# Key and value projections of a two-layer decode step: three one-pass products in place of one fp32 product

## The chip, the cores and the metric

The kernel runs on one core of one Trainium2 chip, as one program. The metric is the device time of one execution in microseconds (us). The engines are TensorE (PE in the profile, its weight loads PEld), VectorE (DVE), ScalarE (ACT), GpSimd (POOL) and SyncE (SP, which here only issues DMAs).

## What is computed

One inference step of a decoder with two layers: a convolution layer, then an attention layer with three branches (compressed, selected, window). There are 512 prompt tokens and 64 sample tokens (8 sequences of 8), so 576 rows of width 1024. Between the layers one key/value set is projected, and that is what the change touches:

```python
def kv_rows(x, g_kv, w_kv):
    h = rms_norm(x, g_kv)
    kv = (h @ w_kv).reshape(x.shape[0], x.shape[1], N_BRANCH, 2, KV_HEADS, HEAD_DIM)
    return kv[:, :, 0], kv[:, :, 1], kv[:, :, 2]
```

`w_kv` is 1024 x 1536: three branches, each 256 columns of keys and 256 of values. The rows of branch 0 are then compressed (windows of 32 tokens through a small network), the keys of branches 1 and 2 are transposed for the scores, all rows are outputs too.

## The kernel before

The program is written by hand, one stream of instructions per engine; the engines wait for each other on counting semaphores, and each executes strictly in its written order. The stages on TensorE are: input projections of the convolution layer (lines 1779 to 1799), statistics and the compression of the past (1801 to 1835), the output projection `row_product` (1871 to 1885), the key/value stage (1888 to 1940), compression of the new rows and first tiles of the query/gate projection (1942 to 1976), the attention loop (2059 to 2070) and the end (2073 to 2171).

**Two kinds of matrix product.** Operands typed fp32 go through `product` (line 1679); an fp32 matmul appears in the trace as two records. The large projections of both layers are done in another way: each operand is split into a high part (an ACT copy into a tile typed fp32r) and a low part (whole minus high, on DVE or POOL, in place), and three fp32r matmuls are added: high x high, high x low, low x high (`split_rows`, lines 1693 to 1701). An fp32r matmul appears as one record.

**The key/value stage.** `w_kv` comes in six chunks of 256 columns (1 MB each): chunk c belongs to branch c // 2, keys where c is even, values where odd. There are five row groups t: four of 128 prompt tokens, and t = 4 with the 64 sample tokens. Job n (loop of line 1899) is one chunk and one row group: 8 fp32 matmuls with 128 stationary token columns of `hT` and 256 moving columns of the chunk, into a half bank of PSUM. In branch 0 the tokens are taken with a step of two. The two t = 4 jobs of a branch are done together (line 1922). The order is by branch, then chunk, then row group; ten jobs per branch, thirty in all. ACT copies each result out of PSUM (line 978), starts the output DMAs after each branch (989 to 997), and at n = 10 copies `u_hi`. PE may run six jobs ahead of these copies.

**The transposes.** `kt_transposes(br)` turns the keys of a branch (two 128x128 transposes per row group, into banks 6 and 7 in turn); branch 1 comes behind job 23, branch 2 behind the last job. Then come 16 transposes of the compressed branch's rows (`ctp_tr`, line 1936), which DVE copies into `ctP` (line 1410), and then `compress_p(0, 1)`, which waits for `ctp_ready` 4 and `kv_ready` 30.

**What comes before.** For each t, `row_product(t)` (four chunks of 8 fp32 matmuls) is followed by a chain over ACT and DVE: squares, root, scale, residual, squares, root, `xn_b` (lines 911 to 937 and 1340 to 1377). PE turns `xn_b` of row group t-1 behind the product of t (`turn_b`), and DVE makes `hT` and `uT` from it (line 1365).

**Loads.** SP issues the weight chunks in one fixed order (line 525 on) and waits before each until its place is free. Chunks 0 and 1 of `w_kv` lie in places 4 and 5 of a ring of six; chunks 2 to 5 take places that hold the output projection's weights, so SP waits for `o_mm` 5, the end of `row_product(4)`. The first query/gate tiles take the places of `w_kv` chunks in turn.

Of the kernel before, what the change touches and what calls it, by code (L numbers as in the profile page):

```python
# [27 lines left out]
P = 128  # L28
# [39 lines left out]
def build(nc, I, O):  # L68
    ctx = ExitStack()
    with ctx:  # L70
# [66 lines left out]
        hT = at(R_H, KD, NT)  # L137
# [18 lines left out]
        scaled_b = at(R_F + 4096, D)  # L156
# [9 lines left out]
        ctP = at(R_G, 2, 8, KV, 32)  # L166
# [14 lines left out]
        wgate_hi = over("wgate_hi", R_Z + 3200, KD, 48)  # L181

        k_stage = at(R_Z, 2, TT, CH)
# [102 lines left out]

        def rows_slot(n):
# [45 lines left out]
        def kv_at(c, t):  # L333


            return 10 * (c // 2) + (4 * (c % 2) + t if t < 4 else 8 + c % 2)
# [43 lines left out]
        for n in range(6):  # L380
            last_use[C_KV + n] = ("kv_mm", kv_at(n, 4) + 1)
# [12 lines left out]
        kv_jobs = {kv_at(c, t): (c, t) for c in range(6) for t in range(TT)}  # L394
# [16 lines left out]
        def chunk_sb(c):  # L411
            return ring[:, place[c][0] // (2 * D)]
# [18 lines left out]
        def rows(t):  # L431
            return P if t < 4 else NS

# [54 lines left out]
        def _(sp):  # L488
# [96 lines left out]
            def new_v_rows(n):  # L585
                b, br = n // 2, n % 2
                sp.dma_start(vnew[:, n % 6], v_sb[NS + DS * b:NS + DS * b + DS, br, 4, :]).then_inc(slot_in[n % 6], 16)
# [38 lines left out]
        def _(pool):  # L626
# [64 lines left out]
            for kind in range(2):  # L691
                for b in range(DB):
                    pool.dma_start(O["win_sample"][b, PAST:KS, kind].rearrange("t k d -> t (k d)"),
                                   (v_sb if kind else k_stage)[kind * NS + DS * b:kind * NS + DS * b + DS, 1, 4]).then_inc(S["late"], 16)
# [44 lines left out]
        def _(act):  # L739
# [170 lines left out]

            for t in range(TT):
# [30 lines left out]
            def split_hi(j):  # L942

                if j == 1:
                    act.wait_ge(S["wg_in"], 16)
                    act.wait_ge(S["o_mm"], TT)
                    copy(wgate_hi, wgate).then_inc(S["hi_ready"], 1)
                    return
                i = j - (j > 1)
                act.wait_ge(slot_in[i % TRING], arrived[C_Q + i])  # L950
                if i >= HRING:
                    act.wait_ge(S["tile_mm"], tile_done(i - HRING))
                copy(tile_hi[:, i % HRING], tile_w[:, i % TRING]).then_inc(S["hi_ready"], 1)

            for n in range(30):
                br, (c, t) = n // 10, kv_jobs[n]
                kind = c % 2
                if n == 10:
# [8 lines left out]
                p0 = kind * NS if t == 4 else 0  # L967
                here = slice(p0, p0 + rows(t))
                act.wait_ge(S["kv_mm"], n + 1)
                src = pb(kv_bank(n), CH)[here]  # L970
                if br == 0 and t < 4:
                    dst = cmp_rows[:, t // 2, kind, :, HD * (t % 2):HD * (t % 2) + HD]
                    src = src.rearrange("p (k d) -> p k d", d=HD)
                elif br == 0:
                    dst = cmp_rows_s[here, kind * CH:(kind + 1) * CH]
                else:
                    dst = (v_sb if kind else k_stage)[here, br - 1, t]
                copy(dst, src).then_inc(S["kv_ready"], 1)
                if n % 10 < 9:
                    continue  # L980

                act.wait_ge(S["kv_ready"], n + 1)
                for kind in range(2):
                    here = slice(kind * NS, kind * NS + NS)
# [11 lines left out]
                    if br == 1:  # L996
                        act.dma_start(O["slc_sample"][:, :, kind].rearrange("b t k d -> (b t) (k d)"), R[here, 0, 4]).then_inc(S["kv_out"], 16)
            split_hi(2)
# [201 lines left out]
        def _(dve):  # L1200
# [138 lines left out]

            for t in range(TT + 1):  # L1340
# [15 lines left out]
                if t:  # L1356
# [7 lines left out]
                    for q, T in enumerate((hT, uT)):  # L1364
                        V.tensor_tensor(out=T[:, :, k * P:k * P + rk], in0=pb(4 + 2 * (k % 2), KD, P)[:, :, 0:rk],
                                        in1=gain(4 + q, rk), op=ALU.mult).then_inc(S["hu_ready"], 1)
                if t < TT:
# [8 lines left out]
                    if t == 1:  # L1376
                        sample_scale()

            def split_lo(j):

                dve.wait_ge(S["hi_ready"], C_OA + j + 1)
# [4 lines left out]
                V.tensor_tensor(out=tile_lo[:, j % TRING], in0=tile_w[:, j % TRING], in1=tile_hi[:, j % HRING],  # L1386
# [7 lines left out]

            for n in range(2 * TT):
                if n == TT:
                    split_lo(0)
                    split_lo(1)
# [7 lines left out]
            dve.wait_ge(S["cs_mm"], 6)  # L1406
            for n in range(4):
                c, gi = n // 2, n % 2
                dve.wait_ge(S["ctp_tr"], n + 1)
                V.tensor_copy(ctP[:, c, :, :, 16 * gi:16 * gi + 16].rearrange("p j k c -> p k c j"),  # L1410
                              pb(6 + n % 2, KV, 16, 8)).then_inc(S["ctp_ready"], 1)
# [262 lines left out]
        def _(pe):  # L1674
# [34 lines left out]
            def tile_product(b0, j):  # L1709
                i = j - (j > 1)  # L1710
                pe.wait_ge(S["lo_ready"], j + 2)
                return split_product(b0, tile_hi[:, i % HRING], tile_lo[:, i % TRING])
# [175 lines left out]
            def kt_transposes(br):  # L1888
                for t in range(TT):
                    n = TT * br + t  # L1890
                    r = rows(t)
                    pe.wait_ge(S["kv_ready"], kv_at(2 * br + 2, t) + 1)
                    if n >= 2:
                        pe.wait_ge(S["kt_ready"], n - 1)
                    for p in range(2):
# [3 lines left out]
            for n in range(30):  # L1899
                c, t = kv_jobs[n]  # L1900
                await_chunk(C_KV + c)
# [10 lines left out]
                if t < 4:  # L1912
                    if c < 2:
                        lhs = hT[:, :, (t // 2) * 256 + t % 2:(t // 2) * 256 + 256:2]
                    else:
                        lhs = hT[:, :, t * P:(t + 1) * P]
                    product(pb(kv_bank(n), CH), ((lhs[:, k], chunk_sb(C_KV + c)[:, k]) for k in range(KD))).then_inc(S["kv_mm"], 1)
                elif c % 2:

                    for k in range(KD):  # L1920
                        for kind in range(2):
                            ins = pe.matmul(pb(kv_bank(n - 1 + kind), CH, p0=kind * NS, p1=kind * NS + NS), hT[:, k, SEQ:NT],
                                            chunk_sb(C_KV + c - 1 + kind)[:, k], start=(k == 0), stop=(k == KD - 1))
                            if k == KD - 1:
                                ins.then_inc(S["kv_mm"], 1)
                if n == 23:
                    kt_transposes(0)
            kt_transposes(1)
            for n in range(4):
                c, gi = n // 2, n % 2  # L1930
                if n >= 2:
                    pe.wait_ge(S["ctp_ready"], n - 1)
                else:
                    pe.wait_ge(S["kt_ready"], 2 * TT)
                for kv in range(KV):
                    ins = pe.transpose(pb(6 + n % 2, KV, P)[:, kv], cmp_rows[:, gi, c, kv], ident)
                ins.then_inc(S["ctp_tr"], 1)

            pe.wait_ge(S["kv_ready"], 30)
# [10 lines left out]
            compress_p(0, 1)  # L1950
            pe.wait_ge(S["hidp_ready"], 2)
# [9 lines left out]
            pe.wait_ge(S["lo_ready"], 3)  # L1961
# [16 lines left out]
            def tile_part(part):  # L1978
# [4 lines left out]
                for k in ks:  # L1983
                    if k == 0:
                        if (i, hf) in bank_clear:
                            pe.wait_ge(S[bank_clear[i, hf][0]], bank_clear[i, hf][1])
                        pe.wait_ge(S["lo_ready"], i + 3)
                    w_hi, w_lo = tile_hi[:, i % HRING, k], tile_lo[:, i % TRING, k]
# [214 lines left out]
```

## Time and profile before

| | us |
|---|---|
| three runs | 987.19, 990.16, 990.83 (median 990.16) |
| the profiled execution's own time | 992.36 |
| its span in the trace | 990.5 |
| PE / DVE / ACT / POOL busy | 923.6 / 511.0 / 424.1 / 302.2 |
| mean granted TensorE clock | 0.986 of full speed |

The profile shows one execution; the trace gives each instruction's start and duration in us from the start of the span. A chain view follows the work that ended last back to what released it; along it, a stretch of matmuls is shown with the time by which they advance. The record of a single matmul is longer than the distance between two, since they are pipelined; the distance is what counts.

### The profile page before, as it was taken

To read this page: it belongs to the slowest core of one execution; us is meant where nothing else is said; L and a number is where in the kernel's file an instruction comes from. 1 tells how busy PE (TensorE), PEld (TensorE's weight loads), DVE (VectorE), ACT (ScalarE), POOL (GpSimd) and SP (SyncE) were. 2 spreads that over 40 slices of the span, in tenths; PEclk is the share of its full clock that TensorE was granted. 3 is DMA by queue.
4 is the path that set the end of the run, shared out by engine and by line. 5 is a ranking of instruction groups with operands and counts; after the bars stand their busy time and mean duration, and the time that the engine had idled before them with its cause. 6 is when DMAs were issued, how large, how long until landed. Compare 5 with 4: busy or idle time off the path is not lost.

```text
span 990.5 us, 16977 instructions
## 1 busy us (share of the span) xinstructions
PE 923.6 (93%) x6398; PEld 788.4 (80%) x6398; DVE 511.0 (52%) x1162; ACT 424.1 (43%) x884; POOL 302.2 (31%) x311
## 2 busy tenths in 40 slices
PE   2799999998999999998989999999999999799996
PEld 2699999944379878876988988989898989686663
DVE  2477999965842450212224545554555545635553
ACT  4456676623412321211334555554554645523411
POOL 0269888771460000003002333233232323400000
PEclk9999999999999999999989999999999999999997
DMA  8345442157336142234532232222232100922521
GB/s 213 85 111 164 117 113 76 49 173 260 143 103 227 43 147 64 48 96 108 133 87 43 65 65 66 43 65 46 62 87 44 44 1 15 269 93 89 170 76 32
DMA packets 156071, 97.44 MB, mean 98 GB/s; under 512 B 97156, under 2 KB 144932, under 8 KB 155911
## 3 DMA queue, kind: packets, MB, share of 16 engines
q1 hardware_dynamic: 141134, 77.07, 29.2%
q0 software_dynamic: 4896, 10.32, 3.0%
q10 hardware_dynamic: 9961, 8.97, 2.7%
q8 instruction: 52, 0.85, 0.4%
q14 instruction: 28, 0.23, 0.1%
HBM read 87.48 MB, written 18.85 MB: 107 GB/s over the span
## 4 chain that ended last, share of the span: by engine, by line
PE 83%; DVE 4%; ACT 4%; SPq 4%; DMA 3%; issue 2%; ACTq 0%; POOL 0%; DVEq 0%
PE psum L1679 17%; PE psum L1989 7%; PE psum L1698 6%; PE psum L1699 6%; PE psum L1700 6%; PE psum L1990 6%; PE psum L1991 6%; PE psum L2084 5%; PE psum L2054 4%; PE psum L2019 3%; PE psum L2037 3%; PE psum L1771 3%; ACT arena L1124 2%; SPq L531 2%; DMA arena<-in_cmp_w 2%
## 5 line engine op out<-in xcount | busy, mean ns | idle before, releaser
L1679 PE MATMUL psum<-arena 128*128 128x256 f32 (+2 forms) x832 | 168.9, 364 | 1.2 <-issue 1.2
L1679 PEld LDWEIGHTS psum<-arena 128*128 128x128 f32 (+1 forms) x832 | 144.8, 187 | 22.6 <-issue 2.3
L741 ACT ACTIVATE arena<-psum 128x512 f32<-128x512 f32 (+9 forms) x214 | 83.6, 434 | 167.5 <-PE psum L1679 59.1
L1989 PE MATMUL psum<-u_hi,tile_hi 128*128 128x288 f32 x464 | 146.5, 316 | 8.6 <-ACT arena L741 8.4
L720 POOL TENSOR_SCALAR arena<-arena,kept 128x512 f32<-128x512 f32 (+3 forms) x128 | 83.6, 668 | 181.7 <-DVE kept L1545 181.7
L1990 PE MATMUL psum<-u_lo,tile_hi 128*128 128x288 f32 x464 | 137.9, 297 | 0.0
L1991 PE MATMUL psum<-u_hi,tile_lo 128*128 128x288 f32 x464 | 137.0, 295 | 0.0
L1273 DVE SCALAR_TENSOR_TENSOR psum<-arena,psum 128x512 f32<-128x512 f32 x168 | 127.0, 756 | 6.0
L1698 PE MATMUL psum<-h_hi,tile_hi 128*128 128x288 f32 x384 | 115.0, 299 | 4.1 <-DVE tile_lo L1245 4.1
L1699 PE MATMUL psum<-h_lo,tile_hi 128*128 128x288 f32 x384 | 114.5, 298 | 0.0
L1700 PE MATMUL psum<-h_hi,tile_lo 128*128 128x288 f32 x384 | 114.1, 297 | 0.0
L1989 PEld LDWEIGHTS psum<-u_hi,tile_hi 128*128 128x128 f32 x464 | 87.7, 189 | 19.8 <-ACT arena L741 11.4
L1476 DVE COPY arena<-psum 128x512 f32<-128x512 f32 (+3 forms) x72 | 37.0, 514 | 103.1 <-PE psum L2037 100.3
L1124 ACT ACTIVATE arena<-arena,kept 128x512 f32<-128x512 f32 (+3 forms) x128 | 70.4, 551 | 44.5 <-DVE kept L1511 44.5
L1990 PEld LDWEIGHTS psum<-u_lo,tile_hi 128*128 128x128 f32 x464 | 87.9, 189 | 1.7 <-issue 1.7
L1991 PEld LDWEIGHTS psum<-u_hi,tile_lo 128*128 128x128 f32 x464 | 87.6, 189 | 0.0
L1698 PEld LDWEIGHTS psum<-h_hi,tile_hi 128*128 128x128 f32 x384 | 73.2, 191 | 4.2 <-issue 4.2
L1699 PEld LDWEIGHTS psum<-h_lo,tile_hi 128*128 128x128 f32 x384 | 73.5, 191 | 0.0
L1700 PEld LDWEIGHTS psum<-h_hi,tile_lo 128*128 128x128 f32 x384 | 73.4, 191 | 0.0
L644 POOL TENSOR_TENSOR tile_lo<-tile_whole,tile_hi 128x1024 fp32r<-128x1024 f32 x23 | 56.4, 2450 | 29.4 <-ACT tile_hi L741 29.3
L741 ACT ACTIVATE tile_hi<-tile_whole 128x1024 fp32r<-128x1024 f32 x56 | 59.1, 1056 | 6.5 <-PE psum L1700 5.5
L2084 PE MATMUL psum<-arena 128*128 128x256 f32 x256 | 60.2, 386 | 1.3 <-POOL arena L727 1.3
(271 smaller groups left out, 1565.2 us busy)
## 6 DMA issues: line engine op xcount, KB each, us to landing
tile_whole<-in_b_w_in SPq DMA_DIRECT2D x64, 256.0 KB
tile_whole<-in_a_w_in SPq DMA_DIRECT2D x24, 512.0 KB
arena<-in_cmp_w SPq DMA_DIRECT2D x3, 2048.0 KB, 10.1
arena<-in_w_kv SPq DMA_DIRECT2D x6, 1024.0 KB, 12.1
bias_copies<-bias_line POOLq DMA_DIRECT2D x4, 1280.0 KB, 25.2
arena<-in_x_prompt SPq DMA_DIRECT2D x8, 512.0 KB, 10.5
arena<-in_a_w_out SPq DMA_DIRECT2D x4, 1024.0 KB, 16.7
arena<-bias_copies SPq DMA_DIRECT2D x16, 256.0 KB, 3.6
```

The source lines that it names most:

```text
L720: pool.tensor_scalar(L, L, rden[:, stat(n) + k:stat(n) + k + 1], gR[:, i, h:h + 1], ALU.mult, ALU.mult).then_inc(S["pn_ready"], 1)
L741: return nc.scalar.activation(out, in_, ACT.Copy, scale=scale)
L1124: nc.scalar.activation(L, L, ACT.Exp, scale=-1.0, bias=mn[:, k:k + 1], accum_out=den[:, k:k + 1]).then_inc(S["exp_done"], 1)
L1273: V.scalar_tensor_tensor(out=acc_p, in0=glu_p[:, m, w:w + SEQ], scalar=tap, in1=acc_p, op0=ALU.mult, op1=ALU.add).then_inc(S["conv_step"], 1)
L1679: ins = pe.matmul(out, l, r, start=(k == 0), stop=(k == len(pairs) - 1))
L1698: pe.matmul(out, w_hi[:, k], h, start=(k == 0), stop=False)
L1699: pe.matmul(out, w_hi[:, k], l, start=False, stop=False)
L1700: ins = pe.matmul(out, w_lo[:, k], h, start=False, stop=(k == KD - 1))
L1989: pe.matmul(pb(7, HT), w_hi, u_hi[:, k, here], start=(k == 0), stop=False)
L1990: pe.matmul(pb(7, HT), w_hi, u_lo[:, k, here], start=False, stop=False)
L1991: ins = pe.matmul(pb(7, HT), w_lo, u_hi[:, k, here], start=False, stop=(k == KD - 1))
L2084: ins = pe.matmul(pb(4 + 2 * (t % 2), 4, CH)[:, c], yT[:, k, t * P:(t + 1) * P], chunk_sb(C_OB + c)[:, k], start=(k == 0), stop=(k == KD - 1))
```

## The change

- **Products.** A job is now a whole branch (keys and values, 512 moving columns, one full bank) and one row group: 15 jobs, n = 5 x branch + t. Each has for each of the 8 slices of the contraction three fp32r matmuls. The sample rows are no longer done in pairs; keys and values both lie in partitions 0 to 63.
- **Splits.** `hT` becomes `kvh_whole`; ACT makes `kvh_hi`, DVE `kvh_lo`, one row group at a time, inside the loop over the output projection's row groups. Each chunk of `w_kv` (128 x 2048 words) is split the same way: chunks 0 and 1 in iterations t = 2 and 3 of that loop, 2 and 3 at n = 1 and 2 of ACT's copy loop, 4 and 5 at n = 6 and 7.
- **Places.** The high parts lie where `x_sb` was (branch 1), and at the end of R_F and start of R_G (branches 0 and 2). `ctP`, `scaled_b`, `k_stage`, `wgate_hi` and the slots of `tile_hi` move; chunks 2 to 5 now lie in places 0 to 3 in order.
- **Order.** The 16 transposes of compressed rows go behind jobs 5 and 6, the key transposes two groups each behind jobs 11 to 14, the last two behind `compress_p(0, 1)`. ACT's copies `u_hi` move behind ten of the fifteen jobs, DVE's tile splits ahead of the key copies. `compress_p(0, 1)` waits for `kv_ready` 24 and `ctp_ready` 4.

```diff
@@ places
-                i = (4, 5, 3, 0, 1, 2)[c - C_KV] if C_KV <= c < C_Q else c % RING if c < C_KV else c - C_OB
+                i = (4, 5, 0, 1, 2, 3)[c - C_KV] if C_KV <= c < C_Q else c % RING if c < C_KV else c - C_OB
@@ ScalarE
+            def kv_rows_hi(t):
+                act.wait_ge(S["hu_ready"], 2 * (t + 1))
+                act.wait_ge(S["o_mm"], t + 1)
+                here = slice(t * P, t * P + rows(t))
+                copy(kvh_hi[:, :, here], kvh_whole[:, :, here]).then_inc(S["hh_ready"], 1)
+
+            def kv_weight_hi(c):
+                act.wait_ge(place[C_KV + c][2], arrived[C_KV + c])
+                if c >= 4:
+                    act.wait_ge(S["kv_mm"], 5)
+                copy(kvw_hi(c // 2)[:, c % 2], kvw_whole[:, (4, 5, 0, 1, 2, 3)[c]]).then_inc(S["hi_ready"], 1)
...
+                if t >= 2:
+                    kv_rows_hi(t - 2)
+                if t in (2, 3):
+                    kv_weight_hi(t - 2)
+            kv_rows_hi(TT - 2)
+            kv_rows_hi(TT - 1)
...
+            for n in range(3 * TT):
+                br, t = n // TT, n % TT
+                if n == 1:
                     act.wait_ge(S["x1_out"], 16 * TT)
                     act.wait_ge(S["xn_b_ready"], TT)
-                    act.wait_ge(S["hu_ready"], 2 * TT)
+                if n in (1, 2):
+                    kv_weight_hi(n + 1)
+                if n in (6, 7):
+                    kv_weight_hi(n - 2)
+                if n == 2 * TT:
+                    act.wait_ge(S["kv_mm"], 2 * TT)
                     for m in range(KD):
                         copy(u_hi[:, m], uT[:, m]).then_inc(S["uh_ready"], 1)
-                if n == 24:
+                if n == 12:
                     split_hi(0)
                     split_hi(1)
...
@@ VectorE
+                    if t >= 2:
+                        kv_rows_lo(t - 2)
+                    if t in (2, 3):
+                        kv_weight_lo(t - 2)
+                    if t == TT - 1:
+                        kv_rows_lo(TT - 2)
+            kv_rows_lo(TT - 1)
+            for c in range(2, 4):
+                kv_weight_lo(c)
+            for n in range(4):
+                c, gi = n // 2, n % 2
+                dve.wait_ge(S["ctp_tr"], n + 1)
+                V.tensor_copy(ctP[:, c, :, :, 16 * gi:16 * gi + 16].rearrange("p j k c -> p k c j"),
+                              pb(6 + n % 2, KV, 16, 8)).then_inc(S["ctp_ready"], 1)
+            for c in range(4, 6):
+                kv_weight_lo(c)
...
@@ TensorE
+            def three(out, w, x, first, last):
+                pe.matmul(out, w[0], x[0], start=first, stop=False)
+                pe.matmul(out, w[0], x[1], start=False, stop=False)
+                return pe.matmul(out, w[1], x[0], start=False, stop=last)
+
+            for n in range(3 * TT):
+                br, t = n // TT, n % TT
+                pe.wait_ge(S["lo_ready"], 1 + 2 * br + 2)
                 if n == 2:
                     turn_b(TT - 1)
                 if n < 2:
-                    pe.wait_ge(S["hu_ready"], 2 * (n + 1))
                     pe.wait_ge(S["o_scaled"], 4)
                 elif n < 6:
-                    pe.wait_ge(S["hu_ready"], 2 * TT if n >= 4 else 2 * (n + 1))
                     pe.wait_ge(S["o_scaled"], TT)
+                    pe.wait_ge(S["hu_ready"], 2 * TT if n >= 4 else 8)
                 else:
-                    pe.wait_ge(S["kv_ready"], n - 5)
...
+                    pe.wait_ge(S["kv_ready"], 2 * (n - 5))
+                if n < 5:
+                    pe.wait_ge(S["hl_ready"], TT + (2, 2, 4, 4, 5)[n])
+                r = rows(t)
+                tokens = slice((t // 2) * 256 + t % 2, (t // 2) * 256 + 256, 2) if br == 0 and t < 4 else slice(t * P, t * P + r)
+                for k in range(KD):
+                    ins = three(pb(kv_bank(n), 2, CH)[0:r], [h[:, k, tokens] for h in (kvh_hi, kvh_lo)],
+                                [w[:, :, k] for w in (kvw_hi(br), kvw_lo(br))], k == 0, k == KD - 1)
+                ins.then_inc(S["kv_mm"], 1)
+                if n in (5, 6):
+                    ctp_transposes(range(2 * n - 10, 2 * n - 8))
+                if n >= 11:
+                    kt_transposes(range(2 * n - 22, 2 * n - 20))
+            pe.wait_ge(S["kv_ready"], 24)
             pe.wait_ge(S["ctp_ready"], 4)
...
             compress_p(0, 1)
+            kt_transposes(range(8, 10))
+            pe.wait_ge(S["kv_ready"], 30)
             pe.wait_ge(S["hidp_ready"], 2)
```

## Rows read from the trace of the kernel before

**Rows 1.** The chain that ended last, share of the span by engine
```profile
PE 83%; DVE 4%; ACT 4%; SPq 4%; DMA 3%; issue 2%; ACTq 0%; POOL 0%; DVEq 0%
```

**Rows 2.** The chain, 251 to 475: start, us advanced, engine, tile, line, count
```profile
251.77 28.54 PE psum L1771 x64
...
346.53 0.87 PE psum L1860 x8
...
362.38 6.92 PE psum L1679 x32
369.30 0.68 PE psum L1860 x8
369.98 20.92 PE psum L1679 x96
390.91 3.60 PE psum L1922 x32
394.51 27.82 PE psum L1679 x128
422.34 3.60 PE psum L1922 x32
425.94 14.01 PE psum L1679 x64
...
442.10 14.01 PE psum L1679 x64
456.11 3.60 PE psum L1922 x32
...
466.94 7.39 PE psum L1679 x64
```

**Rows 3.** Timeline of PE, one-pass matmuls: start, duration, line, operands, count
```profile
475.88 0.30 PE L1698 MATMUL psum<-u_hi,tile_hi 128*128 128x288 f32 x1
...
481.48 0.30 PE L1698 MATMUL psum<-u_hi,tile_hi 128*128 128x288 f32 x1
...
481.88 0.29 PE L1698 MATMUL psum<-u_hi,wgate_hi 128*48 128x288 f32 x1
...
482.68 0.29 PE L1698 MATMUL psum<-u_hi,wgate_hi 128*48 128x288 f32 x1
...
540.75 0.39 PE L2019 MATMUL psum<-kt_lo,q_hi 64*128 64x512 f32 x2
540.99 0.39 PE L2019 MATMUL psum<-kt_hi,q_lo 64*128 64x512 f32 x2
541.22 0.22 PE L2019 MATMUL psum<-kt_hi,q_hi 64*128 64x128 f32 x2
```

**Rows 4.** Timelines of ACT and DVE: splits of two 128x1024 pieces
```profile
483.67 2.02 ACT L741 ACTIVATE kt_hi<-arena 128x1024 fp32r<-128x1024 f32 x2
...
485.72 2.36 DVE L1424 TENSOR_TENSOR kt_lo<-arena,kt_hi 128x1024 fp32r<-128x1024 f32 x2 [0.67 <-ACT kt_hi L741]
```

**Rows 5.** Timelines of ACT and DVE where row groups 2 to 4 end
```profile
339.64 0.20 ACT L928 ACTIVATE kept<-kept 128x1 f32<-128x1 f32 x1 [0.80 <-DVE kept L1203]
346.56 1.02 ACT L920 ACTIVATE arena<-psum 128x1024 f32<-128x1024 f32 x1 [6.72 <-PE psum L1679]
...
353.24 0.20 ACT L928 ACTIVATE kept<-kept 128x1 f32<-128x1 f32 x1 [0.80 <-DVE kept L1203]
...
368.46 0.74 DVE L1375 TENSOR_SCALAR arena<-arena,kept 64x1024 f32<-64x1024 f32 x1
```

**Rows 6.** Windows: bounds, us, busy PE, PEld, DVE, ACT, POOL; clock, DMA share, GB/s
```profile
370.00:375.00 5.00, 5.00 (x24) 4.55 (x25) 1.29 (x2) 0.39 (x1) 0.53 (x1) 1.00 1.12 348
375.00:380.00 5.00, 5.00 (x25) 4.55 (x24) 0.00 (x0) 0.39 (x1) 0.00 (x0) 1.00 0.29 78
```

**Rows 7.** Timeline of ACT's queue: output DMAs issued behind branch 0
```profile
395.36 2.11 ACTq L989 DMA_DIRECT2D out_cmp_prompt<-arena  x4
...
400.51 0.56 ACTq L990 DMA_DIRECT2D out_cmp_sample<-arena  x1
```

More of the change, by code:

```diff
@@ L165, in build @@
         ctS = at(R_G, 8, 33, 16)
-        ctP = at(R_G, 2, 8, KV, 32)
+        ctP = at(R_G + 8320, 2, 8, KV, 32)
         cmp_rows = at(R_G + 2048, 2, 2, KV, 2 * HD)
@@ L180, in build @@
         wgate_lo = over("wgate_lo", R_S + 760, KD, 48)
-        wgate_hi = over("wgate_hi", R_Z + 3200, KD, 48)
-        k_stage = at(R_Z, 2, TT, CH)
+        wgate_hi = over("wgate_hi", R_RING + (TRING + HRING) * D + 2 * TT * CH, KD, 48)
+        k_stage = at(R_RING + (TRING + HRING) * D, 2, TT, CH)
+        kvh_lo = over("kvh_lo", R_H, KD, NT)
+        kvh_whole = over("kvh_whole", R_H, KD, NT, dtype=F32)
+        kvh_hi = over("kvh_hi", R_Z, KD, NT)
+        KVW_HI = (R_F + 4608, R_G, R_X, R_X + 2 * D)
+        kvw_low = over("kvw_span", KVW_HI[0], KVW_HI[1] - KVW_HI[0] + 2 * D)
+        kvw_far = bass.AP(kvw_low.tensor, kvw_low.offset, [kvw_low.ap[0], [KVW_HI[1] - KVW_HI[0], 2], [CH, KD], [1, CH]])
+        kvw_near = over("kvw_near", KVW_HI[2], 2, KD, CH)
+        kvw_rest = over("kvw_rest", R_RING, RING, KD, CH)
+        kvw_whole = over("kvw_whole", R_RING, RING, KD, CH, dtype=F32)
         gateT = at(R_Z + 2560, NT)
@@ L285, in kv_bank, with kvw_hi, kvw_lo @@
             return (2, 3, 0, 1, 4, 5)[n % 6]
+        def kvw_hi(br):
+            return kvw_near if br == 1 else kvw_far
+        def kvw_lo(br):
+            first = (4, 0, 2)[br]
+            return kvw_rest[:, first:first + 2]
         def rows_slot(n):
@@ L411, in chunk_sb @@
         def chunk_sb(c):
-            return ring[:, place[c][0] // (2 * D)]
+            return (kvw_whole if C_KV <= c < C_Q else ring)[:, place[c][0] // (2 * D)]
         def chunk_dst(c, how):
@@ L432, in rows, with hi_slot @@
             return P if t < 4 else NS
+        def hi_slot(i):
+            return (i + 2) % HRING
         UPM = 1 + 2 * 2 * 4
@@ L952, in split_hi @@
                     act.wait_ge(S["tile_mm"], tile_done(i - HRING))
[L953 to L958, printed above, removed]
+                copy(tile_hi[:, hi_slot(i)], tile_w[:, i % TRING]).then_inc(S["hi_ready"], 1)
+            for n in range(3 * TT):
+                br, t = n // TT, n % TT
+                if n == 1:
@@ L978, in _ @@
-                copy(dst, src).then_inc(S["kv_ready"], 1)
-                if n % 10 < 9:
+                for kind in range(2):
+                    here = slice(0, rows(t))
+                    src = pb(kv_bank(n), 2, CH)[here, kind]
+                    if br == 0 and t < 4:
+                        dst = cmp_rows[:, t // 2, kind, :, HD * (t % 2):HD * (t % 2) + HD]
+                        src = src.rearrange("p (k d) -> p k d", d=HD)
+                    elif br == 0:
+                        dst = cmp_rows_s[here, kind * CH:(kind + 1) * CH]
+                    else:
+                        dst = (v_sb if kind else k_stage)[here, br - 1, t]
+                    copy(dst, src).then_inc(S["kv_ready"], 1)
@@ L980, in _ @@
+                if t < 4:
                     continue
-                act.wait_ge(S["kv_ready"], n + 1)
+                act.wait_ge(S["kv_ready"], 2 * (n + 1))
                 for kind in range(2):
-                    here = slice(kind * NS, kind * NS + NS)
+                    here = slice(0, NS)
                     if br == 0:
@@ L1338, in sample_scale, with kv_rows_lo, kv_weight_lo @@
                                 op=ALU.mult).then_inc(S["lnx_ready"], 1)
+            def kv_rows_lo(t):
+                dve.wait_ge(S["hh_ready"], TT + t + 1)
+                here = slice(t * P, t * P + rows(t))
+                V.tensor_tensor(out=kvh_lo[:, :, here], in0=kvh_whole[:, :, here], in1=kvh_hi[:, :, here], op=ALU.subtract).then_inc(S["hl_ready"], 1)
+            def kv_weight_lo(c):
+                dve.wait_ge(S["hi_ready"], C_OA + c + 1)
+                V.tensor_tensor(out=kvw_lo(c // 2)[:, c % 2], in0=kvw_whole[:, (4, 5, 0, 1, 2, 3)[c]], in1=kvw_hi(c // 2)[:, c % 2],
+                                op=ALU.subtract).then_inc(S["lo_ready"], 1)
             for t in range(TT + 1):
@@ L1363, in _ @@
                     dve.wait_ge(S["tr_b"], k + 1)
-                    for q, T in enumerate((hT, uT)):
+                    for q, T in enumerate((kvh_whole, uT)):
                         V.tensor_tensor(out=T[:, :, k * P:k * P + rk], in0=pb(4 + 2 * (k % 2), KD, P)[:, :, 0:rk],
@@ L1385, in split_lo @@
                 j -= j > 1
-                V.tensor_tensor(out=tile_lo[:, j % TRING], in0=tile_w[:, j % TRING], in1=tile_hi[:, j % HRING],
+                V.tensor_tensor(out=tile_lo[:, j % TRING], in0=tile_w[:, j % TRING], in1=tile_hi[:, hi_slot(j)],
                                 op=ALU.subtract).then_inc(S["lo_ready"], 1)
@@ L1404, in _ @@
                     V.tensor_copy(kt_new[:, br], pb(6 + n % 2, 2, P)[:, :, 0:NS]).then_inc(S["kt_ready"], 1)
[L1406 to L1411, printed above, removed]
             split_lo(2)
@@ L1885, in _, with kt_transposes @@
                     turn_b(t - 1)
-            def kt_transposes(br):
-                for t in range(TT):
-                    n = TT * br + t
+            def kt_transposes(group):
+                for n in group:
+                    br, t = n // TT, n % TT
                     r = rows(t)
@@ L1894, in kt_transposes @@
                         pe.wait_ge(S["kt_ready"], n - 1)
+                    else:
+                        pe.wait_ge(S["ctp_ready"], n + 3)
                     for p in range(2):
@@ L1897, in kt_transposes, with ctp_transposes @@
                     ins.then_inc(S["kt_tr"], 1)
-            for n in range(30):
-                c, t = kv_jobs[n]
-                await_chunk(C_KV + c)
+            def ctp_transposes(group):
+                for n in group:
+                    c, gi = n // 2, n % 2
+                    if n >= 2:
+                        pe.wait_ge(S["ctp_ready"], n - 1)
+                    else:
+                        pe.wait_ge(S["kv_ready"], 8)
+                    for kv in range(KV):
+                        ins = pe.transpose(pb(6 + n % 2, KV, P)[:, kv], cmp_rows[:, gi, c, kv], ident)
+                    ins.then_inc(S["ctp_tr"], 1)
+            def three(out, w, x, first, last):
[3 more added lines that the diff above has]
+            for n in range(3 * TT):
+                br, t = n // TT, n % TT
+                pe.wait_ge(S["lo_ready"], 1 + 2 * br + 2)
                 if n == 2:
@@ L1926, in _ @@
[L1926 to L1937, printed above, removed]
@@ L1960, in _ @@
             tile_product(0, 0).then_inc(S["tile_mm"], 1)
-            pe.wait_ge(S["lo_ready"], 3)
+            pe.wait_ge(S["lo_ready"], 6 + 3)
+            pe.wait_ge(S["kt_ready"], 2 * TT)
             split_product(6, wgate_hi, wgate_lo).then_inc(S["gate_mm"], 1)
```

52 lines of the change are left out of this document (13 added, 39 removed).

## Prediction, written before the changed kernel was run

> **What bounds the kernel now.** I read the chain that ended last first: TensorE holds 83% of it [rows 1]. In order of time it shows which part of TensorE's work lies in the changed stage [rows 2]. From the first key/value job at 362.38 to the first matmul of `compress_p(0, 1)` at 466.94 there are 104.56 us, and they are made up like this: 24 jobs of 16 records (6.92 + 20.92 + 27.82 + 14.01 + 14.01 = 83.68), three pairs of sample jobs (3 x 3.60 = 10.80), `turn_b(4)` 0.68, the key transposes of branch 1 with their waits (439.95 to 442.10, 2.15), and everything behind the last job (459.71 to 466.94, 7.23). Up to that last piece TensorE hardly waits, so the stage is worth what its matmuls take, and a wait of another engine matters only if the new splits make one. The windows give the granted clock there as 1.00, the level of 2.4 GHz [rows 6].
>
> **The price of a one-pass matmul of 512 columns.** This is the term that decides, and no row shows exactly this form. Three rows come near [rows 3].
> - The same three-way product with 288 moving columns: from 475.88 to 481.48 there are 42 matmuls, 5.60 / 42 = 0.1333 us each. That is 0.463 ns per column, and 512 columns would take 0.237.
> - One-pass matmuls with 512 columns, but with 64 stationary rows and two at a time on the two halves of the array: 540.75, 540.99, 541.22, so 0.235 us per step.
> - Below, 512 columns at one per clock of 2.4 GHz are 0.213.
>
> I take 0.235, the row with the same width. The ends for the range are 0.213 and 0.237. A fp32 record of 256 columns advances 14.01 / 64 = 0.219 us [rows 2], so a job of before (16 records) computes 256 columns in 3.50 us, and a new job (24 records) computes 512 in 5.64. The gain is only that of 24 x 0.235 against 32 x 0.219, not that of one pass against two records each.
>
> The Trainium skill, "TensorE: Matmul & The Clock Gate", section "Back-to-back issue gap", gives two other prices: N / 2.4 + 2.5 ns for a matmul by itself, 216 ns at 512 columns, and about 131 ns for a sustained stream at that width. At 288 columns the first rule gives 122.5 ns where the row has 133.3, so here it is somewhat low. By it the jobs would take 77.7 us, some 7 less than by my row; the second is a rival below.
>
> **The change part by part.**
> - Products: 15 jobs x 24 x 0.235 = 84.6 us in place of 83.68 + 10.80 = 94.48. For the 12 jobs of prompt rows that is 67.7 against 83.7, a gain of 16.0. For the three sample jobs it is 16.9 against 10.8, a loss of 6.1, because the pairs on two halves of the array are given up. Together -9.9 (between -17.7 and -9.2).
> - Behind the last job: the 7.23 us go, with the 2.15 behind branch 1. What remains of them between the jobs are the transposes alone. Eight transposes advance 0.87 us [rows 2], 0.109 each: 16 of compressed rows 1.74, the first eight key groups (seven of two, one of the smaller sample rows) 1.67. In both groups of two behind one job, what the second pair waits for (`kt_ready`, `ctp_ready`) is a copy of an earlier job's pair, 5 us old. So 3.41 in place of 9.38: -5.97. The two last key groups stand behind `compress_p(0, 1)`, where PE waits for ACT's last silu anyway; they cost nothing there, and 0.4 us if that cover is thin.
> - `turn_b(4)` stays, 0.68.
>
> New stage: 84.6 + 0.68 + 3.41 = 88.7 us, against 104.56. **Sum: -15.9 us** (ends: 76.8 gives -23.7, 85.3 gives -15.2).
>
> **The splits beside it.** ACT splits two pieces of 1024 words in 2.02 us and DVE in 2.36 [rows 4]: a chunk of `w_kv` takes 2.0 and 2.4, a row group half of that. Due times against ready times, by the trace's clock:
> - Chunks 0, 1 and rows 0, 1: due at 362.4 for job 0. ACT is through with iteration t = 2 at 339.8, adds 1.0 + 2.0, and meets the next group at 346.6; in t = 3 it is through at 353.4 and adds the same, to 356.5. DVE ends at about 345.3 and 358.9 [rows 5]. 3.5 us to spare, and the chain to `xn_b` isn't pushed.
> - Rows 2, 3: due for job 2 at 362.4 + 11.3 + 0.7 = 374.3. DVE writes the last `xn_b` until 369.2 [rows 5] and then has two low parts, to 371.7. 2.6 us to spare, the tightest one. If it isn't met, PE stands by just what is missing.
> - Rows 4: behind `turn_b(4)`, ready at 376.5 to 377, due at 385.6.
> - Chunks 2 and 3: their loads run from 361.4, and the traffic of the four chunks fades between 375 and 380 [rows 6]. ACT splits them at about 376 to 381, DVE until 384. Due for job 5 at 391.3.
> - Chunks 4 and 5: ACT must first issue the ten output DMAs of branch 0, 5.7 us from 395.36 on in the kernel before [rows 7], from about 392 on in the new one. Queued behind them are job 5's copy and the two splits, to 406; DVE is done by 410, with the `ctP` copies ahead of these. Due for job 10 at 421.2.
> - `u_hi` and the first tiles come from 421 on; who waits for them is `tile_product(0, 0)`, at about 459.
>
> SP is moved nowhere; the first tiles wait for job 10 of 15 instead of 20 of 30, the same place. The second load of `w1_sb` is bound to `compress_p(0, 1)` and shifts with it. Behind 466.94 no instruction changes but the places of `tile_hi`, so what is gained moves the end.
>
> **The rivals.**
> - *Splits come late.* A low part is missing where a branch or job 2 starts. For: PE now depends on two engines' in-order streams, in which splits stand behind output DMAs and copies. Against: the distances above. With every split at twice its price, rows 2 and 3 come 2.5 us late and chunk 3 is just met. Price 3 to 10 us: 977 to 984.
> - *The gain is given back behind the stage*, at the start of the attention loop, which waits for output DMAs and the bias loads. For: they have 16 us less of PE work in front of them than in absolute time. Against: all are issued from events inside the stage and shift with it. If half is lost: 982.
> - *Slower: the weight loads stop hiding.* Each of the 360 matmuls loads its own 128 stationary columns, in branch 0 with a step of two. If a load of 0.19 us (the record's length) no longer ran beside the stream of 0.21, a matmul would take 0.40, the jobs 144 us, and the kernel 1034. It decides from (104.56 - 4.09) / 360 = 0.279 us per matmul on. Against: with 48 stationary columns (481.88 to 482.68, six matmuls) the distance is again 0.133 [rows 3], so the load isn't what sets it; and the farthest-spread operands of the trace, the 495 columns of line 1771, go at 28.54 / 64 = 0.446 us per record, 8% over their 990 clocks [rows 2].
> - *The change doesn't do what it says*: a 512-column fp32r matmul runs as two records like fp32. Then a matmul takes 2 x 0.219 = 0.438, the jobs 158 us, and the kernel 1047. The 512-column rows speak against it.
> - *Much faster*: matmuls of a dense stream overlap, so that 512 columns cost no more than 288 do, 0.133: jobs 48 us, kernel 938. No row with the whole array goes below its columns at 2.4 GHz. By the skill's 131 ns (same page and section) it would be the same time; this trace doesn't bear it out.
>
> **How the numbers follow.** The profiled execution took 992.36 us, 2.2 more than the median of the runs; 992.36 - 15.9 = 976.5 for such an execution, 990.16 - 15.9 = **974.3** for the median. Chances: forecast 0.77, splits late 0.12, given back 0.05, weight loads 0.03, two records 0.01, much faster 0.02. The low end is 990.16 - 23.7 = 966.5, the high end 975.0 plus 6 us of late splits, 981. Over 0.5% faster is below 985.2, which covers the first three cases but for a small part: faster 0.92, same 0.04, slower 0.04. (A half per cent is about what a measurement of this kernel can tell from no change.)
>
> **What would show it.** 360 one-pass matmuls of a new form at 0.235 us, jobs of 5.6 us; the first matmul of `compress_p(0, 1)` near 451; no idle time of PE in front of jobs 0, 2, 5 and 10; records of line 1679's `product` down by 384. A distance under 0.22 or over 0.25 would make the sum wrong; so would a wait on DVE's low parts in front of job 2, or a gap in front of the attention loop that is larger than it is now.

## The result and the profile after

The changed kernel takes 974.63 us (median of 4 runs, 972.98 to 976.04), the kernel before beside it 990.50 (4 runs, 987.19 to 993.23). The ratio is 0.9825, 95% interval 0.9806 to 0.9845. The prediction was 974.3 with a range of 966.5 to 981. The profiled execution took 973.55 us, its span is 971.4.

The chain that ended last, in the changed kernel (excerpt): start, us advanced, engine, tile, line, count. Lines 1975 to 1977 are the three one-pass products, 1922 is `turn_b`, 1971 the transposes of compressed rows, 1960 those of keys, 1741 is `product`.

```profile
358.84 1.02 PE psum L1922 x8
359.86 0.24 PE psum L1975
...
370.97 0.64 PE psum L1922 x8
...
394.05 0.87 PE psum L1971 x8
...
400.53 0.87 PE psum L1971 x8
...
429.32 0.44 PE psum L1960 x4
...
435.27 0.44 PE psum L1960 x4
...
441.26 0.63 PE psum L1960 x4
...
447.44 0.44 PE psum L1960 x4
447.88 7.14 PE psum L1741 x64
```

From the first job at 359.86 to the first matmul of `compress_p(0, 1)` at 447.88 there are 88.02 us, where before there were 104.56 [rows 2]: 16.5 less. The transposes that made blocks of 2.15 and 7.23 us stand alone between jobs. Nothing waits inside the stage. These are all the waits of TensorE between 355 and 505, and all three lie behind 447.88 (the engine and line that waited, the releaser, us, times, longest):

```profile
PE psum L2073 <- issue: 3.7, 1, 3.7
PE psum L2056 <- ACT arena L761: 0.5, 1, 0.5
PE psum L1741 <- ACT arena L1049: 0.5, 1, 0.5
```

The distance of the one-pass matmuls with 512 columns, from TensorE's timeline of the changed kernel (start, duration, line, operands, stationary shape, moving shape):

```profile
372.33 0.39 PE L1975 MATMUL psum<-kvw_span,kvh_hi 128*128 128x512 f32 x1
...
382.04 0.39 PE L1975 MATMUL psum<-kvw_span,kvh_hi 128*128 128x512 f32 x1
...
382.73 0.39 PE L1975 MATMUL psum<-kvw_span,kvh_hi 128*64 128x512 f32 x1
...
387.58 0.39 PE L1975 MATMUL psum<-kvw_span,kvh_hi 128*64 128x512 f32 x1
388.28 0.39 PE L1975 MATMUL psum<-kvw_near,kvh_hi 128*128 128x512 f32 x1
...
393.19 0.40 PE L1975 MATMUL psum<-kvw_near,kvh_hi 128*128 128x512 f32 x1
```

42 matmuls from 372.33 to 382.04 are 0.2312 us each, 21 with only 64 stationary columns (382.73 to 387.58) 0.2310, and 21 of branch 1 (388.28 to 393.19) 0.2338. Over all 360 the mean is 0.2325 (83.7 us of jobs, worked out below). Before, 288 columns took 0.133 and 512 on half the array 0.235 [rows 3]: the new form is next to that second row.

The splits end ahead of their use. VectorE's low parts in the changed kernel, from its timeline:

```profile
353.70 2.29 DVE L1390 TENSOR_TENSOR kvw_rest<-kvw_whole,kvw_span 128x2048 fp32r<-128x2048 f32 x1 [0.58 <-ACT kvw_span L761]
...
366.70 2.36 DVE L1386 TENSOR_TENSOR kvh_lo<-kvh_whole,kvh_hi 128x1024 fp32r<-128x1024 f32 x2
...
375.98 4.64 DVE L1390 TENSOR_TENSOR kvw_rest<-kvw_whole,kvw_near 128x2048 fp32r<-128x2048 f32 x2 [1.66 <-ACT kvw_near L761]
...
402.90 4.48 DVE L1390 TENSOR_TENSOR kvw_rest<-kvw_whole,kvw_span 128x2048 fp32r<-128x2048 f32 x2
```

Chunk 1 is ready at 356.0 and used at 359.9; rows 2 and 3 at 369.1, used at 371.6; chunks 2 and 3 at 380.6, used at 388.3; chunks 4 and 5 at 407.4, used at 418.1.

**The rest of the span.** The two spans differ by 19.1 us, 2.6 more than the stage. Behind the stage they agree: 990.5 - 466.94 = 523.56 before, 971.4 - 447.88 = 523.52 after. The 2.5 us lie ahead of it, at the second compression of the past, whose 64 matmuls the change doesn't touch. In the changed kernel's chain:

```profile
236.27 14.63 DMA arena<-in_cmp_w
250.95 26.84 PE psum L1833 x64
```

Before, the same load runs from 236.00 and the matmuls start at 251.77 and take 28.54 us [rows 2]. So 0.8 us are a later start, because the load took 1.1 us longer, and 1.7 us are slower matmuls. The windows of that place say why they are slower (bounds, us, busy PE, PEld, DVE, ACT, POOL, granted clock, DMA share, GB/s). First the kernel before:

```profile
251.00:258.00 7.00, 6.23 (x11) 2.78 (x12) 6.81 (x7) 4.13 (x6) 1.25 (x1) 0.76 0.84 317
```

and the changed one:

```profile
251.00:258.00 7.00, 7.00 (x17) 3.28 (x18) 6.96 (x8) 4.15 (x6) 0.95 (x1) 1.00 0.91 339
```

In the one execution the clock was granted at its level of 1.2 GHz for a while, in the other it stayed at 2.4. Ahead of these matmuls TensorE waits for the load, and not equally long: in the kernel before, the changed kernel, the run with transposes only and the run with one product of three, in this order,

```profile
PE psum L1771 <- DMA arena<-in_cmp_w: 2.3, 1, 2.3
PE psum L1833 <- DMA arena<-in_cmp_w: 2.2, 1, 2.2
PE psum L1772 <- DMA arena<-in_cmp_w: 3.2, 1, 3.2
PE psum L1833 <- DMA arena<-in_cmp_w: 3.6, 1, 3.6
```

Of the nine profiles, the three with waits of 2.3, 3.2 and 3.6 us have 28.54 us for the 64 matmuls. Five with waits of 2.0 to 2.2 us have 26.84, and the one with no wait there (fp32 products) 26.57. One of the three slow ones has the changed layout. That the 2.5 us are scatter of the executions and no effect of the change is argued from the medians: they differ by 15.9, near the stage's 16.5 and not near 19.1.

### The profile page after: what moved, and what is told of

It reads as the page before. It is cut to its first block, busy times and chain, and to the rows that moved or that the text cites. A ratio compares the mean times of both kernels' runs of the same rounds, so it can differ in the third digit from the quotient of the medians.

```text
span 971.4 us, 16757 instructions
## 1 busy us (share of the span) xinstructions
PE 908.4 (94%) x6278; PEld 771.1 (79%) x6278; DVE 530.2 (55%) x1173; ACT 437.2 (45%) x895; POOL 301.2 (31%) x311
## 4 chain that ended last, share of the span: by engine, by line
PE 84%; SPq 4%; DVE 3%; ACT 3%; DMA 3%; issue 2%; ACTq 0%; POOL 0%; DVEq 0%
PE psum L1741 9%; PE psum L2056 7%; PE psum L1760 6%; PE psum L1761 6%; PE psum L1762 6%; PE psum L2057 6%; PE psum L2058 6%; PE psum L2151 5%; PE psum L2121 4%; PE psum L2086 4%; PE psum L2104 3%; PE psum L1976 3%; PE psum L1975 3%; PE psum L1977 3%; PE psum L1833 3%; SPq L551 2%
## 5 line engine op out<-in xcount | busy, mean ns | idle before, releaser
L1741 PE MATMUL psum<-arena 128*128 128x256 f32 (+2 forms) x448 | 84.7, 350 | 0.0
L1741 PEld LDWEIGHTS psum<-arena 128*128 128x128 f32 (+1 forms) x448 | 71.5, 183 | 11.5 <-issue 0.2
```

What stands on the lines that cost most here:

```text
L1741: ins = pe.matmul(out, l, r, start=(k == 0), stop=(k == len(pairs) - 1))
```

## The experiments

The theory is that of the prediction. The stage costs what TensorE's instructions in it cost, one after the other: the number of one-pass matmuls times their 0.2315 us, plus the transposes, as long as each split is ready when it is due. The rivals: the spreading of the transposes brought most of the gain; the splits set the pace; the gain comes from wide jobs and not from the one-pass form; matmuls of a dense stream overlap, so that their number counts for less. The kernel before had a median of 991.06 us beside four of the runs (transposes alone, products alone, doubled splits, sample rows side by side) and of 993.08 beside the other three, so it is the ratios that compare.

**The transposes alone,** in the kernel before:

```diff
-                if n == 23:
-                    kt_transposes(0)
-            kt_transposes(1)
...
+                if n in (11, 13):
+                    ctp_transposes(range(n - 11, n - 9))
+                if n in (21, 23, 25, 27):
+                    kt_transposes(range(n - 21, n - 19))
...
             compress_p(0, 1)
+            kt_transposes(range(8, 10))
```

(Left out are the removed loop of the 16 transposes of compressed rows and VectorE's copies of the results, which follow the new order.)

> The kernel before with its fp32 jobs, where only the transposes are spread: compressed rows behind jobs 11 and 13, two groups of keys each behind jobs 21, 23, 25 and 27, the last two behind compress_p(0, 1). If the terms of my sum add up: of the 9.38 us behind the jobs 3.41 remain, and about 0.9 more, because the last two jobs lie in the PSUM banks that the compression writes, so that it must wait for their copies. That is 5.1 us less: ratio 0.9949, stage (first key/value job to first matmul of the compression) 99.5 us. The rival, that the transposes only cost something because they stand behind slow copies which now delay the jobs instead: within 1 us of before, stage over 103.

Measured: 984.72 us, ratio 0.9934 (0.9913 to 0.9955), stage from 362.52 to 462.07, 99.55 us, so 5.0 less, where 5.1 were expected. The terms add up, the wait for the banks included, as the end of its chain shows:

```profile
457.60 3.65 PE psum L1936 x32
461.26 0.36 ACT arena L741
461.64 0.39 ACT arena L741
462.07 7.41 PE psum L1680 x64
```

**The products alone,** in the changed kernel, with the transposes in two blocks again:

```diff
-                if n in (5, 6):
-                    ctp_transposes(range(2 * n - 10, 2 * n - 8))
-                if n >= 11:
-                    kt_transposes(range(2 * n - 22, 2 * n - 20))
-            pe.wait_ge(S["kv_ready"], 24)
+                if n == 11:
+                    kt_transposes(range(TT))
+            kt_transposes(range(TT, 2 * TT))
+            ctp_transposes(range(4))
+            pe.wait_ge(S["kv_ready"], 30)
```

> The changed kernel with its one-pass products and splits, but with the transposes in the two blocks where they were before. Terms that add up: the jobs stay at 83.1 us, the two blocks cost their 9.38 again instead of 3.41, so the stage is 93.9 and the kernel 6 us slower than the changed one: 980.6, ratio to before 0.990. If instead spreading the transposes brought most of the gain, it is within 2 us of before.

Measured: 979.51 us, ratio 0.9896 (0.9863 to 0.993). The stage is 359.78 to 453.43, 93.65 us: 5.6 more than in the changed kernel and 10.9 less than before. So of the 16.5 us two thirds are the products and one third the transposes. The two parts measured alone, 5.0 and 10.9, make 15.9. The missing 0.6 goes with the first run's wait of 0.9 us for banks, which the changed kernel doesn't have: only with 15 jobs do the last ones leave the banks of the compression free.

**Every split twice:**

```diff
+                copy(kvh_hi[:, :, here], kvh_whole[:, :, here]).then_inc(S["twice_a"], 1)
+                twice[0] += 1
+                act.wait_ge(S["twice_a"], twice[0])
                 copy(kvh_hi[:, :, here], kvh_whole[:, :, here]).then_inc(S["hh_ready"], 1)
...
+                place_c = kvw_whole[:, (4, 5, 0, 1, 2, 3)[c]]
+                link(dve, V.tensor_tensor(out=place_c, in0=place_c, in1=place_c, op=ALU.max))
                 V.tensor_tensor(out=kvw_lo(c // 2)[:, c % 2], ...
```

> The changed kernel, with every split of the key/value operands done twice on both engines (ACT copies twice, DVE has a pass of the same size ahead of each subtraction). If only the due times count, nothing is lost until a low part comes late. By the changed kernel's timeline the second chunk is then ready at 363.6 where job 0 is due at 359.9: 3.8 us of waiting in front of job 0, and up to 0.5 in front of jobs 2 and 5, so 4 us in all, 978.6, ratio 0.988, not the 22 us or so that the doubled work takes on ACT and again on DVE. If the splits are what paces the stage, 15 us or more.

Measured: 980.28 us, ratio 0.9898 (0.9867 to 0.9929). The one wait is where it was expected, and 4.0 us instead of 3.8; the 0.5 us in front of jobs 2 and 5 didn't come:

```profile
PE psum L1986 <- DVE kvw_rest L1401: 4.0, 1, 4.0
```

But the stage is 94.96 us (360.14 to 455.10), 6.9 more and not 4. The rest is the clock. TensorE's timeline behind the wait:

```profile
364.15 0.80 PE L1986 MATMUL psum<-kvw_span,kvh_hi 128*128 128x512 f32 x1 [4.01 <-DVE kvw_rest L1401]
364.74 0.63 PE L1987 MATMUL psum<-kvw_rest,kvh_hi 128*128 128x512 f32 x1
...
369.86 0.46 PE L1987 MATMUL psum<-kvw_rest,kvh_hi 128*128 128x512 f32 x1
370.16 0.39 PE L1988 MATMUL psum<-kvw_span,kvh_lo 128*128 128x512 f32 x1
```

and the windows of the same run:

```profile
360.00:364.10 4.10, 0.14 (x2) 0.00 (x0) 4.07 (x3) 0.44 (x2) 0.00 (x0) 0.89 0.92 308
...
366.00:368.00 2.00, 2.00 (x6) 1.59 (x5) 2.00 (x2) 0.28 (x1) 0.00 (x0) 0.50 1.10 348
...
370.00:372.00 2.00, 2.00 (x10) 1.67 (x9) 0.89 (x2) 1.97 (x3) 0.00 (x0) 1.00 1.11 365
```

During the idle 4.0 us the granted clock fell to half, 1.2 GHz, and it came back near 370. Twelve matmuls from 364.74 to 369.86 took 0.427 each instead of 0.231, which is 2.4 us; the first one's longer start and the one at 369.86 add 0.4, which makes 2.8 of the 2.9. The Trainium skill, "TensorE: Matmul & The Clock Gate", section "Why this matters for your kernels", says to avoid idle gaps of TensorE between bursts of matmuls. This row agrees. The theory held (the doubled work costs nothing but its one wait and what that leaves behind), and the price of a wait that I had used was too low.

**Two products of three, and one of three:**

```diff
                 pe.matmul(out, w[0], x[0], start=first, stop=False)
-                pe.matmul(out, w[0], x[1], start=False, stop=False)
-                return pe.matmul(out, w[1], x[0], start=False, stop=last)
+                return pe.matmul(out, w[0], x[1], start=False, stop=last)
```

(the second run keeps the first matmul alone)

> The changed kernel without the product of the low part of the rows and the high part of the weights (its outputs lack that small term): 240 matmuls in place of 360, all splits kept. If TensorE's count of matmuls is the stage, 120 x 0.2315 = 27.8 us go. The jobs are then 3.7 us and catch up with the splits: by the changed kernel's timeline about 1.2 us of waiting in front of job 2, 0.4 in front of job 5 and 1 for the key copies behind job 12, so 25 us less than the changed kernel, 949.5, ratio 0.958. If matmuls in a dense stream overlap, so that a third of them is worth much less than a third of the time, 15 us or less.

Measured: 948.62 us, ratio 0.9557 (0.9539 to 0.9574; 0.958 was expected), stage 62.5 us (360.3 to 422.83), 25.5 less than in the changed kernel. Two of the three expected waits are there, and the 0.4 in front of job 5 isn't:

```profile
PE psum L1975 <- DVE kvh_lo L1386: 1.3, 1, 1.3
PE psum L1960 <- DVE arena L1470: 1.1, 1, 1.1
```

So a third of the matmuls is worth the full third, 27.8 us less the waits of 2.4. The rival of matmuls that overlap (15 us or less) is ruled out.

> The changed kernel with only the product of the high parts (its outputs are those of one rounded product): 120 matmuls in place of 360, all splits kept. By the count alone 55.6 us would go, down to 919. The jobs are then 1.85 us, and the splits are the bound: waits of about 3 us in front of job 2 (last rows), 3.6 in front of job 5 (second chunk pair), 1.2 in front of job 10, 4.7 for the key copies, 13 in all, so 932 us, and more where TensorE's clock falls after such a wait, as it did in the run with doubled splits. If the splits had much more room than I read from the timeline, near 919.

Measured: 937.03 us beside a kernel before at 993.08, ratio 0.9431 (0.9416 to 0.9447); 933.8 on the scale of 990.16. The stage is 50.0 us. Counting alone would give 88.0 - 55.6 = 32.4, so 17.6 us are waits and what they leave behind:

```profile
PE psum L1960 <- DVE arena L1470: 5.7, 1, 5.7
...
PE psum L1922 <- issue: 3.2, 1, 3.2
...
PE psum L1975 <- DVE kvw_rest L1390: 2.3, 2, 1.3
PE psum L1975 <- DVE kvh_lo L1386: 1.3, 1, 1.3
```

```profile
366.00:368.00 2.00, 0.23 (x2) 0.00 (x0) 2.00 (x2) 1.15 (x2) 0.00 (x0) 1.00 1.09 349
...
370.00:372.00 2.00, 0.67 (x7) 0.51 (x5) 2.00 (x3) 0.29 (x1) 0.00 (x0) 0.50 1.07 382
```

These make 12.5 us. They stand at the expected places and not all with the expected length: around job 2 there are 3.2 in front of `turn_b(4)` (line 1922), which I hadn't listed, and 1.3 behind it, 4.5 where I had 3; in front of job 5 1.3 instead of 3.6, of job 10 1.0 instead of 1.2, and 5.7 for the key copies instead of 4.7. The remaining 5.1 us stand in stretches at half clock behind the two longest waits: the 24 matmuls of jobs 2 to 4 took 7.46 us instead of 5.55, and the 8 behind the 5.7 us

```profile
406.08 3.41 PE psum L1975 x8
```

instead of 1.85. That is 3.5; the rest, the turn and the transposes in the same stretches included, I didn't separate. Here the splits are the bound, with a third of the matmuls. In the changed kernel they aren't, and with two thirds they begin to be.

**fp32 products of 512 columns,** in the changed kernel's order:

```diff
-                    ins = three(pb(kv_bank(n), 2, CH)[0:r], [h[:, k, tokens] for h in (kvh_hi, kvh_lo)],
...
+                    first = (4, 0, 2)[br]
+                    ins = pe.matmul(pb(kv_bank(n), 2, CH)[0:r], kvh_whole[:, k, tokens], kvw_whole[:, first:first + 2, k],
+                                    start=(k == 0), stop=(k == KD - 1))
```

> The changed kernel's order, loads and transposes with fp32 products: each job is 8 fp32 matmuls of 512 columns, the splits are left out (one-element instructions stand for them). It tells the one-pass form from the rest of the change. A fp32 matmul is two records of 512 columns; at the rate of the 256-column ones (0.2185 for 256, so 0.437) a job takes 7.0 us and 15 take 105, sample jobs included, which are no pairs. Stage 109 us, 21 us slower than the changed kernel: 995.7, ratio 1.005 to before. If it is the width of 512 columns or the removed splits that brings the gain, it is near 975.

Measured: 995.92 us (10 runs) beside 993.08 (13 runs), ratio 1.0028 (1.0012 to 1.0045; 1.005 was expected). Its chain has the stage as a few long pieces:

```profile
359.55 13.74 PE psum L1996 x32
...
373.93 28.01 PE psum L1996 x64
...
410.56 34.68 PE psum L1996 x80
445.68 6.87 PE psum L1996 x16
...
460.48 7.01 PE psum L1996 x16
```

The pieces give 0.429 to 0.438 us a record; with the two not shown (6.87 each, at 402.82 and 452.98) they add up to 104.05 us for 240 records, 0.434 each, 6.94 a job, and the stage to 108.5. So width alone gains little: 0.434 against 2 x 0.219 = 0.438 for the same columns, 0.4 us over the prompt jobs. The loss on the unpaired sample jobs, 3 x (6.94 - 3.60) = 10.0 us, is larger than that and the 5.6 of the spread transposes together, which is why this stage is 4.0 longer than before. Without the one-pass form nothing of the change's gain is left; with it, the shares are those of the runs above, two thirds for the products and one third for the transposes.

**Sample rows side by side.** The three sample jobs were the term that spoke against the change: +6.1 us in the sum. As a pair on two halves of the array they weren't tried in the one-pass form. Another form uses what the rows showed, that 64 stationary columns cost the same as 128. High and low parts of the 64 sample rows are put side by side as one stationary operand; two matmuls per slice (with the high and the low weights) then give all products, that of low part and low part among them, which the other form leaves out. ACT copies one half of the result, DVE adds the other.

```diff
+                    if t < 4:
...
+                        continue
+                    pe.matmul(pb(kv_bank(n), 2, CH), kvh_two[:, k], kvw_hi(br)[:, :, k], start=(k == 0), stop=False)
+                    ins = pe.matmul(pb(kv_bank(n), 2, CH), kvh_two[:, k], kvw_lo(br)[:, :, k], start=False, stop=(k == KD - 1))
...
-                    kt_transposes(range(2 * n - 22, 2 * n - 20))
+                    kt_transposes(((0, 1), (2, 3), (4,), (5, 6, 7))[n - 11])
...
+                        copy(sample_dst(br, kind), pb(kv_bank(n), 2, CH)[NS:P, kind]).then_inc(S["half_ready"], 1)
...
+                    V.tensor_tensor(out=sample_dst(br, kind), in0=sample_dst(br, kind),
+                                    in1=pb(kv_bank(5 * br + 4), 2, CH)[0:NS, kind], op=ALU.add).then_inc(S["kv_ready"], 1)
```

> The changed kernel, with the sample jobs in another form: the high and the low part of the 64 sample rows lie side by side as one stationary operand of 128 columns, so that two matmuls per slice (times the high and times the low weights) do what three did; the two halves of PSUM are added by ACT and DVE. If a matmul costs its 512 moving columns whatever the stationary width, 24 of 360 matmuls go: 24 x 0.2315 = 5.6 us less than the changed kernel, with up to 0.4 back for a transpose that waits: 969.3, ratio 0.979. If a matmul with 128 stationary columns costs more than one with 64, or the sums over two engines come late for the copies behind them, less than 2 us.

Measured: 969.04 us (966.9 to 970.68, 4 runs) beside 991.06, ratio 0.9785 (0.9753 to 0.9818). The stage is 83.04 us (359.85 to 442.89), 5.0 less than in the changed kernel. A sample job now takes 3.69 us, sixteen matmuls of 0.231:

```profile
382.72 0.39 PE L2018 MATMUL psum<-kvw_span,kvh_two 128*128 128x512 f32 x1
...
386.41 0.39 PE L1993 MATMUL psum<-kvw_near,kvh_hi 128*128 128x512 f32 x1
```

and the one new wait is the expected one, of a key transpose behind the last job, where three groups stand instead of two:

```profile
PE psum L1978 <- DVE arena L1488: 0.4, 1, 0.4
```

This version is faster than the kernel before. Against the changed kernel the intervals of the two ratios just overlap (0.9806 to 0.9818); every execution of it was faster than every one of the changed kernel (970.68 at most against 972.98 at least), and the stage in the two traces shows the difference directly.

## Why the prediction was right

- **The matmul.** The term that decided was taken as 0.235 us; the mean of the 360 is 0.2325. Jobs: 88.02 less 0.64, 1.74 and 1.95 of turns and transposes makes 83.7 us, where 84.6 were forecast. Row and form differed in two ways (half the array, two at a time), and that they would make so little difference was assumed and not shown beforehand. The rule N / 2.4 + 2.5 ns of the Trainium skill ("TensorE: Matmul & The Clock Gate", section "Back-to-back issue gap"), 216 ns, is 15 ns low here. Its 131 ns for a sustained stream of 512 columns doesn't occur in any run.
- **The transposes.** Sum 3.41 forecast, 3.69 measured: 2 x 0.87 for the compressed rows, as forecast, and 0.44 + 0.44 + 0.63 + 0.44 for the keys. The 0.28 too much is the one pair behind job 13 that contains the sample rows; it takes 0.63 in the runs with transposes only, with doubled splits and with fp32 products too, and no run tells why. The saving of 5.97 is 5.6 in the run with products only. That `compress_p(0, 1)` no longer waits came out as said.
- **Due times.** All five held, to within half a us of my table (chunk 1 3.9 us ahead where I had 3.5, rows 2 and 3 2.5 where I had 2.6, chunk 5 10.7 where I had 11).
- **Behind the stage** nothing was given back: 523.56 and 523.52.
- **The rivals.** The weight load stays hidden: with 64 and 128 stationary columns the distance is 0.2310 and 0.2312 in branch 0. One argument against this rival was misread. The 8% over 990 clocks at line 1771 are mostly not the operands' doing: a part of those 28.54 us ran at half clock, and in the changed kernel the same 64 records take 26.84, 0.419 each, 1.7% over. The one-pass form is one record, and dense matmuls don't overlap below their columns (two products of three).
- **Where a step was wrong:** the text took a late split to cost PE "just what is missing". The doubled splits show that a wait of 4.0 us costs 6.9, while waits of 1.3 and 1.1 us cost just themselves. In that rival's price of 3 to 10 us this was covered by the range, but not understood. It also put the wait with doubled splits at rows 2 and 3 and chunk 3; it is in front of job 0, where DVE's doubled work pushes back the chain of row group 3 as well and ends at 364.1. I had checked each split against its own slack and not the sum along DVE's stream.
- **What was luck:** the forecast and the median agree to 0.3 us, while the stage itself got 16.5 us shorter and not 15.9 (jobs 0.9 too dear, transposes 0.3 too cheap), and the profiled spans differ by 19.1. The scatter of the executions, 2.5 us of it at one place ahead of the stage, is several times that agreement.

## What to carry to other kernels

Three one-pass products cost four fifths of a fp32 product here (24 x 0.231 = 5.5 us against 32 x 0.219 = 7.0 for 512 columns), and that only where the form is otherwise the same; what the new form gives up, here pairs of small jobs on two halves of the array, must go into the sum with it. When stationary width costs nothing, fill it: high and low parts of a short row group side by side save a third of its matmuls. And add up an engine's new work along its whole stream against the due times; a due time that is missed by 4 us cost 7 here, since TensorE's clock fell meanwhile.

## What the runs showed of the hardware

- A one-pass (fp32r) matmul: 0.133 us at 288 columns, 0.231 at 512, with 64 or 128 stationary columns. A fp32 record: 0.219 at 256 columns, 0.434 at 512.
- The same matmul is 1.1% slower in branch 1 (0.2338), whose high weights lie in another place. No run tells whether the place is the cause; the run with products only shows it too (0.234), the one with two products of three doesn't (0.227 to 0.230).
- After 4.0 us without work TensorE's clock was granted at 0.50, and matmuls took 0.427 instead of 0.231 us for about 5 us. After waits of 1.3 and 1.1 us (two products of three) it wasn't. At the second compression of the past it fell in the three profiles with waits of 2.3, 3.2 and 3.6 us and not in the five with 2.0 to 2.2. The kernel before, with its 2.3 us, had also been granted less than the full clock a little earlier (0.71 from 240 to 244); what decides between 2.2 and 2.3 us stays open.
- ACT copied PSUM partitions 64 to 127 into partitions 0 to 63 of SBUF (in the run with sample rows side by side, at 386.61, 0.66 us for two pieces of 64 x 256), and DVE then added the lower half (at 387.02, 0.74 us for the two).
